# Turning the hidden activations of two MLPs: TensorE transposes against 16-bit transposing DMAs in SBUF

## The reference

```python
def sq_relu_mlp(xn, w_up, w_down):
    return jnp.square(jax.nn.relu(xn @ w_up)) @ w_down

for l in range(DEPTH):
    hn = rms_norm(h, mix_norm_g[l])
    h = h + (diff_hgrn_mixer(...) if l % 2 == 0 else short_conv_mixer(...))
    hn = rms_norm(h, mlp_norm_g[l])
    h = h + sq_relu_mlp(hn, mlp_w_up[l], mlp_w_down[l])
```

## Time and profile before

| | before |
|---|---|
| median of 3 runs (lowest to highest) | 2233.13 us (2233.05 to 2233.82) |
| the profiled execution's own time | 2233.02 us |
| its span (first to last instruction) | 2231.3 us |
| TensorE busy | 2218.5 us, 99% |
| VectorE, ScalarE, GpSimd busy | 82%, 60%, 13% |
| mean granted clock of TensorE | 0.999 |

### The profile page before, as it was taken

How to read it: one execution, slowest core, us unless ns; L and a number is a source line. 1 busy time by engine, 2 the same in 40 slices (tenths; PEclk the granted TensorE clock), 3 DMA queues, 4 the chain that set the end, 5 groups by cost and what they waited for, 6 DMA issues and landing times.

```text
span 2231.3 us, 29958 instructions
## 1 busy us (share of the span) xinstructions
PE 2218.5 (99%) x10290; PEld 1842.1 (83%) x10290; DVE 1831.9 (82%) x1922; ACT 1349.7 (60%) x1708; POOL 290.7 (13%) x413
## 2 busy tenths in 40 slices
PE   9999999999999999999999999999999999999998
PEld 8888888888888888888888888888888888888887
DVE  5778888866888888888876999886888888888886
ACT  6555555537666666666666566565665665665664
POOL 4444555520000000000000000000000000000000
PEclk9999999999999999999999999999999999999999
DMA  9555555566779678678656878757686796796755
GB/s 280 160 167 152 155 164 150 151 180 217 210 250 274 196 248 274 198 246 274 198 170 236 244 227 247 230 159 251 190 293 194 233 293 193 231 296 194 231 180 170
DMA packets 326408, 479.96 MB, mean 215 GB/s; under 512 B 13929, under 2 KB 145810, under 8 KB 319634
## 3 DMA queue, kind: packets, MB, share of 16 engines
q1 hardware_dynamic: 318322, 423.88, 58.0%
q0 software_dynamic: 7344, 53.48, 12.9%
q10 hardware_dynamic: 624, 1.07, 0.1%
HBM read 422.79 MB, written 2.10 MB: 190 GB/s over the span
## 4 chain that ended last, share of the span: by engine, by line
PE 95%; DVE 2%; issue 1%; POOL 1%; ACT 1%; SPq 0%; DMA 0%; POOLq 0%; DVEq 0%; ACTq 0%
PE pair L483 21%; PE pair L485 20%; PE pair L493 20%; PE m L1192 9%; PE m L1183 9%; PE m L1186 9%; PE m L1246 1%; DVE w_lo L599 1%; PE m L1022 1%; PE m L1084 1%; PE m L948 1%; DVE raw L1973 0%; PE m L1036 0%; PE m L1047 0%; PE m L1266 0%
## 5 line engine op out<-in xcount | busy, mean ns | idle before, releaser
L593 ACT ACTIVATE w_hi<-raw 128x1024 fp32r<-128x1024 f32 x796 | 814.4, 1055 | 583.4 <-DVE raw L1973 301.1
L599 DVE TENSOR_TENSOR w_lo<-raw,w_hi 128x1024 fp32r<-128x1024 f32 x796 | 940.1, 1219 | 217.5 <-ACT w_hi L593 213.6
L483 PE MATMUL pair<-w_hi,yT_hi 128*128 128x512 f32 x1264 | 496.2, 393 | 0.0
L485 PE MATMUL pair<-w_hi,yT_lo 128*128 128x512 f32 x1264 | 492.2, 389 | 0.0
L464 DVE TENSOR_TENSOR w_lo<-raw,w_hi 128x1024 fp32r<-128x1024 f32 x208 | 256.0, 1254 | 117.9 <-ACT w_hi L451 116.9
L451 ACT ACTIVATE w_hi<-raw 128x1024 fp32r<-128x1024 f32 x208 | 218.4, 1060 | 221.7 <-PE pair L485 217.1
L493 PE MATMUL pair<-w_lo,yT_hi 128*128 128x512 f32 x1264 | 338.1, 389 | 0.0
L483 PE MATMUL pair<-w_hi,xT_hi 128*128 128x512 f32 x832 | 329.8, 396 | 0.0
L485 PE MATMUL pair<-w_hi,xT_lo 128*128 128x512 f32 x832 | 324.3, 390 | 0.0
L493 PEld LDWEIGHTS pair<-w_lo,yT_hi 128*128 128x128 f32 x1264 | 237.2, 188 | 49.7
L483 PEld LDWEIGHTS pair<-w_hi,yT_hi 128*128 128x128 f32 x1264 | 237.3, 188 | 48.2 <-issue 0.3
(11 more groups left out here) (192 smaller groups left out, 2284.8 us busy)
## 6 DMA issues: line engine op xcount, KB each, us to landing
raw<-in_mlp_w_up SPq DMA_DIRECT2D x128, 1024.0 KB, 7.1
raw<-in_mlp_w_down SPq DMA_DIRECT2D x256, 512.0 KB, 6.4
raw<-in_ab_w_in SPq DMA_DIRECT2D x256, 256.0 KB, 4.1
raw<-raw POOLq DMA_DIRECT2D x51, 1024.0 KB, 8.6
raw<-in_conv_w_in SPq DMA_DIRECT2D x32, 1024.0 KB, 7.0
raw<-in_ab_w_out SPq DMA_DIRECT2D x64, 256.0 KB, 4.5
raw<-in_conv_w_in SPq DMA_DIRECT2D x32, 512.0 KB, 5.7
raw<-in_conv_w_out SPq DMA_DIRECT2D x32, 512.0 KB, 5.8
```

The source lines that it names most:

```text
L483: nc.tensor.matmul(dst[:, tt], at(hi, kt, tt), w_hi[:, ring, q], start=begin, stop=False)
L485: mm = nc.tensor.matmul(dst[:, tt], at(lo, kt, tt), w_hi[:, ring, q], start=False, stop=False)
L593: nc.scalar.activation(w_hi[:, entry % HALVES], src, ACT.Copy).then_inc(hi_ready, 1)
L599: nc.vector.tensor_tensor(w_lo[:, entry % HALVES], src, w_hi[:, entry % HALVES].bitcast(F32), ALU.subtract).then_inc(lo_ready, 1)
```

## The change

The pairs are no longer turned by TensorE. Each block is turned on its own, in SBUF:
- `turn` moves to ScalarE, right after a block's square. An ACTIVATE with Copy reads the block as 16-bit halves of its 32-bit words and writes all lower halves, then all upper halves (`parts`, 128 x 1024 elements of 16 bits). ScalarE waits for its own write and issues one transposing DMA of 128 x 1024 16-bit elements from `parts` to `turned_parts`.
- `hidden_hi` (ScalarE) waits for that DMA, puts the halves together again with a second ACTIVATE (`whole`), waits for that, and rounds the 128 x 512 block into yT_lo's space. The high parts are now in yT_lo and the low parts in yT_hi, as `parts` and `whole` lie over yT_hi, `turned_parts` over yT_lo.
- `hidden_lo` (VectorE) is one subtraction of 128 x 512 per block, from SBUF.
- The places: turn at X3 (C11), X4 (C21, after `hidden_hi` of C11), before round 1 (C12, C22), and at D3, D4, D5, D6 of each round. `hidden_hi` at X4 and X5 ahead of the splits, then in P1 (and D0 in round 1), P4, P2, D7 behind the splits. `hidden_lo` in D5, D6, D7 and the next P1. `copy` of C21 moves from P4, behind the splits, to D4, ahead of the split.
- The waits on c_T are now on c_parts (laid apart). The wait of P2 for c_lo is gone.

The core of the diff:

```diff
-                def turn(r, pair_of):            # TensorE
-                    for at, c in enumerate(pair_of):
-                        n = made(st, r, c)
-                        pe.wait_ge(c_sq, n)
-                        if at == 0 and n > 1:
-                            pe.wait_ge(c_lo, n - 1)
...
-                        for q in range(4):
-                            ins = nc.tensor.transpose(M[turn_bank(r, c)][:, q * P:(q + 1) * P],
-                                                      c_block(st, c)[:, q * P:(q + 1) * P], ident[:])
-                        ins.then_inc(c_T, 1)
...
-                def hidden_hi(r, pair_of):
-                    eng.wait_ge(c_T, made(st, r, pair_of[1]))
-                    low = "C11" if "C11" in pair_of else "C12"
-                    nc.scalar.activation(hidden(yT_hi, r, low), turned_pair(r, low), ACT.Copy
-                                         ).then_inc(c_hi, 2)
+                def turn(r, c):                   # ScalarE
+                    n = made(st, r, c)
+                    eng.wait_ge(c_sq, n)
+                    nc.scalar.activation(
+                        parts(r, c).rearrange("p (s k) -> p s k", s=2),
+                        c_block(st, c).bitcast(U16).rearrange("p (k s) -> p s k", s=2), ACT.Copy
+                        ).then_inc(c_parts, 1)
+                    eng.wait_ge(c_parts, n)
+                    eng.dma_start_transpose(
+                        turned_parts(r, c).rearrange("p (a b) -> p a b", b=P), parts(r, c)
+                        ).then_inc(c_turned[n % 2], 16)
+                def hidden_hi(r, c):
+                    n = made(st, r, c)
+                    eng.wait_ge(c_turned[n % 2], 16 * ((n + 1) // 2))
+                    nc.scalar.activation(
+                        parts(r, c).rearrange("p (k s) -> p s k", s=2),
+                        turned_parts(r, c).rearrange("p (s k) -> p s k", s=2), ACT.Copy
+                        ).then_inc(c_whole, 1)
+                    eng.wait_ge(c_whole, n)
+                    nc.scalar.activation(hidden(yT_lo, r, c), whole(r, c), ACT.Copy
+                                         ).then_inc(c_hi, 1)
...
                     elif p == 3:
                         wait_product(eng, at + 3, 0, 0)
                         square(0, "C11")
+                        turn(0, "C11")
                         square(0, "C21")
+                    if p == 4 and st != CONV:
+                        hidden_hi(0, "C11")
+                        turn(0, "C21")
+                    if p == 5 and st != CONV:
+                        hidden_hi(0, "C21")
...
                 square(0, "C12")
+                turn(0, "C12")
                 square(0, "C22")
+                turn(0, "C22")
...
-                        if name == ("P5" if r == 1 else "D0"):
-                            hidden_hi(r - 1, ("C12", "C22") if r == 1 else ("C21", "C11"))
+                        if name == "D4":
+                            copy(r, "C21")
                         split(slot + 2)
                         if name[0] == "P":
                             split(slot + 3)
-                        if name == "P4":
-                            hidden_hi(r, ("C22", "C12"))
-                            copy(r, "C21")
+                        if name == "P1":
+                            hidden_hi(r - 1, "C12" if r == 1 else "C11")
+                        if name == "D0" and r == 1:
+                            hidden_hi(0, "C22")
+                        if name in ("P4", "P2", "D7"):
+                            hidden_hi(r, {"P4": "C22", "P2": "C12", "D7": "C21"}[name])
...
                         if name in ("D3", "D4", "D5", "D6"):
                             square(r, {"D3": "C22", "D4": "C12", "D5": "C21", "D6": "C11"}[name])
-                hidden_hi(ROUNDS - 1, ("C21", "C11"))
+                            turn(r, {"D3": "C22", "D4": "C12", "D5": "C21", "D6": "C11"}[name])
+                hidden_hi(ROUNDS - 1, "C11")
```

More of the change, by code:

```diff
@@ L30 @@
 U32 = mybir.dt.uint32
+U16 = mybir.dt.uint16
 ALU = mybir.AluOpType
@@ L169, in build @@
             in_y = beside[:, KT * T // 2:]
+            in_y_hi = beside[:]
         yT_hi = sb("yT_hi", [P, KT, T], F32R)
+        with nc.sbuf_tensor("beside_lo", [P, KT * T], F32) as beside_lo:
+            in_y_lo = beside_lo[:]
         yT_lo = sb("yT_lo", [P, KT, T], F32R)
@@ L566, in part_of, with block_at, whole, parts @@
             return half // 2, slice(2 * (half % 2), 2 * (half % 2) + 2)
+        def block_at(r, block):
+            return 4 * (r % 2) + (0 if block in ("C11", "C21") else 2) + int(block in ("C21", "C22"))
         def hidden(tile, r, block):
[L570 to L582, removed]
+            at = 512 * block_at(r, block)
+            return tile.rearrange("p a b -> p (a b)")[:, at:at + 512]
+        def whole(r, block):
+            at = 512 * block_at(r, block)
+            return in_y_hi[:, at:at + 512]
+        def parts(r, block):
+            return whole(r, block).bitcast(U16)
+        def turned_parts(r, block):
+            at = 512 * block_at(r, block)
+            return in_y_lo[:, at:at + 512].bitcast(U16)
+        def hidden_at(tile, kt, tt):
+            at = 512 * (kt // 4 * 2 + tt) + P * (kt % 4)
+            return tile.rearrange("p a b -> p (a b)")[:, at:at + P]
         def c_block(st, block):
@@ L1301, in stage @@
                              p % 4 == 0, p % 4 == 3)
-                    if p == 5 and st != CONV:
-                        turn(0, ("C11", "C21"))
                 if st == CONV:
@@ L1331, in stage @@
                             down(r, int(name[1]))
-                        if name == ("D0" if r == 1 else "P1"):
-                            turn(r - 1, ("C12", "C22") if r == 1 else ("C21", "C11"))
-                        if name == "P4":
-                            turn(r, ("C22", "C12"))
-                turn(ROUNDS - 1, ("C21", "C11"))
                 for m in range(8):
@@ L1590, in stage @@
                         squares(norm, (2 * p - 2, 2 * p - 1))
-                    if p == 6 and st != CONV:
-                        hidden_hi(0, ("C11", "C21"))
                     split(at + p + 2)
@@ L2133, in stage @@
                         sum_squares(norm)
-                    if p == 6 and st != CONV:
-                        hidden_lo(0, ("C11", "C21"))
+                    if p in (5, 6) and st != CONV:
+                        hidden_lo(0, ("C11", "C21")[p - 5])
                     if p == 7 and st == CONV:
```

49 lines of the change are left out of this document (23 added, 26 removed).

## The result

The changed kernel is slower: 2326.97 us median of 4 runs (2325.78 to 2330.25) against 2233.18 of the kernel before in the same session, a ratio of 1.0421 with a 95% interval of 1.0408 to 1.0434. I had forecast 2244 us with a range of 2214 to 2315. The sign was right, the size was not.

The account below looks back on a forecast made before the run. TensorE's own list of work was taken as the bound. Per stage -14.4 (turns) + 4.6 (start) + 7.0 (round 1) + 6 x 1.4 (rounds) = +5.6, two stages +11 on 2233.0: 2244 us, range 2214 to 2315.

Parts of the forecast that it names:

- What bounds it, and the direction: Whole kernel: TensorE's own list of work bounds it, a late ScalarE makes VectorE then TensorE late; slower at 0.60.
- Turns removed, 28.8 us: TensorE, both stages: 32 pairs of blocks at 0.9 us each leave its list, if it never waits.
- Laying apart 1.06: ScalarE, per block: the 16-bit strided ACTIVATE of 1024 elements takes 1.06 us, like a w_hi half.
- Laying together 1.06: ScalarE, per block: the copy that puts the halves together again takes 1.06 us.
- Rounding 0.58: ScalarE, per block: rounding to yT_lo after the halves are put together takes 0.58 us.
- Issue 0.86: ScalarE, per block: issuing the transposing DMA holds it 0.86 us, with 0.34 and 1.66 as ends.
- rival 2: ScalarE's queue: the issue holds it 1.66 us or more and ScalarE becomes the bound, 2293 us; chance 0.32.
- D5, 1.2 lost: Each steady round at D5's first half: ScalarE has 3.6 us more ahead, against a margin of 2.4, 1.2 lost.
- D6 to P5 fits: Each steady round, D6 to P5: two turns and three blocks laid together need 9.1 of ScalarE's 13.1 us idle.
- Landing 6.4, hidden in rounds: Transposing DMA: lands 6.4 us from issue; C21's and C11's transfers have about 12 us in a round, so hidden.
- rival 3: Transposing DMAs: landing is the bound at 10.9 us or more, blocks queuing with weight loads, 2264 us; chance 0.08.
- The granted clock at 1.00: TensorE: granted clock left at 1.00, though stops of 3 us are twice the trace's longest.

Follow-up runs that it names:

- bare copies: Changed kernel without any DMA, the laying apart made one 32-bit ACTIVATE of 128x512 and the laying together left out: 2219.5 us, ratio 0.9938.
- second pair without a DMA: Changed kernel with the transposing DMAs of C21 and C11 left out in rounds 1 to 7: 2300.7 us, ratio 1.0297.

## Why the prediction was wrong

By spans, the 94.3 us between before (2231.3) and after (2325.6) are: turns removed, with bare copies, -13.6; 16-bit copies +21.1; transfers on SyncE's queue +6.9, at the stage starts, round 1 and the ends; the issue on ScalarE instead of SyncE +79.9.

1. *What bounds it, and the direction*: right. A late ScalarE made VectorE and TensorE late, at the places named: X6, D0 of round 1, D5. Over half of TensorE's 82 us of idle time are waits for w_hi.
2. *Turns removed, 28.8 us*: a pair is 0.9 us of TensorE's list as I had it (a round's matmuls alone are 81.6). What failed is that the gain arrives: P6 took back 0.9 a round in the bare kernel, where I had 0.2, because I priced the wait by its idle time alone. A stop also delays the matmuls behind it by some 0.3 us: at D5 the second comes 2.03 us late (1001.30, where matmuls 0.23 us apart would have had it at 999.27), of which the idle time is 1.75.
3. *Laying apart 1.06*: right, 1.058. *Laying together 1.06*: mis-sized, 1.36; it writes in steps of two elements, the other only reads so. *Rounding 0.58*: 0.63.
4. *Issue 0.86*: this is the step that decided. It takes 1.25 us, with the pause behind it 1.38. I took the row of the nearest route, GpSimd's; but that was another engine and a plain pattern, and the number that I kept as an end (1.66) was no farther off. From 1.1 up my own rival 2 was to hold, and it does. What it lost before the turns are taken off was 4.6 us a round, 10.4 in round 1, 6.1 at the start and 0.5 at the end; measured in the same way (0.9 us added per pair) it is 6.4, 12.7, 3.9 and 4.5, so its start was too dear and all else too cheap.
5. *D5, 1.2 lost*: 1.75 idle and 0.3 behind it. The formula was fair: with the measured 1.06 + 0.03 + 1.38 it gives 1.9 + 0.48 + 2.47 - 0.25 - 2.4 = 2.2.
6. *D6 to P5 fits*: false. The second pair without a DMA shows 1.2 us a round, most of it the stop in P5. I had compared sums of work with sums of idle time, 9.1 against 13.1 us; by my own terms it is 9.0 (two turns of 1.95, three times 1.7), and in rival 2 10.6 plus a backlog of 5 would overflow 13.1 by 2.5, where I had 1.5 without a reason. VectorE's work ahead of the sums for P5 counts as well: with its subtraction on GpSimd the 0.28 us stop in P5 is gone and a round is 0.7 us shorter (both with the issue on SyncE), while a later half of P5 still starts 0.53 us behind the matmul before it, as in the other. That a delay of VectorE there is paid in full is argued and not shown.
7. *Landing 6.4, hidden in rounds*: right, 7.0. The longest is 13.9. ScalarE waits for a landing four times in all, 3.9 and 3.8 us in X4 and 0.6 and 1.0 at the ends, so rival 3 is out. The estimate of 10.5 us from the page "VectorE: DVE Perf Modes" of the Trainium skill is not borne out: a block of eight squares lands in 7.0, one of four in 6.1 and the plain transfer in 6.1.
8. *The granted clock at 1.00*: wrong after some of the stops. TensorE around 2.03 us without a matmul at X6, and the window of it with the granted clock as the third number from the right:

```profile
565.11 1.07 PE L499 MATMUL pair<-w_lo,xT_hi 128*128 128x512 f32 x4
568.21 0.68 PE L489 MATMUL pair<-w_hi,xT_hi 128*128 128x512 f32 x1 [2.03 <-ACT w_hi L457]
568.68 0.63 PE L491 MATMUL pair<-w_hi,xT_lo 128*128 128x512 f32 x1
569.11 0.63 PE L489 MATMUL pair<-w_hi,xT_hi 128*128 128x512 f32 x1
...
567.00:572.00 5.00, 3.79 (x10) 3.01 (x11) 3.74 (x4) 4.97 (x7) 0.00 (x0) 0.66 0.05 10
```

Matmuls start 0.43 us apart instead of 0.23, which is the level of 1.2 GHz, for some 3.5 us, and the window's granted clock is 0.66. The same follows the 3.9 us stop at D0 of round 1. The length of the stop does not decide alone. In this trace the clock fell in six places: after stops of 2.03, 3.89, 1.82, 3.99, 1.78 and 3.63 us. It stayed at its upper level (1.00) after one of 2.03 us at 647.91, one of 3.43 at 1208.48, and those of 1.7 to 1.85 us at D5 of rounds 2 to 7. Over the whole span the granted clock is 0.994 against 0.999, which makes 0.005 x 2326 = some 12 us of the 94 at most, an estimate, a term that I had set to zero though the stops were in my own sum. With the issue on SyncE it is 0.999 again.

So the step that failed is the issue's length (0.86 for 1.25 to 1.38), which put the case on the side of rival 2; the P5 stretch, the price behind a stop and the clock made it larger still (2327 against the 2293 that I had for that rival). Moving the issue alone gives 79.9 of the 94.3 us back. The form of the loss, a late ScalarE at the places named, was right; the direction was too, though I gave the case that came only 0.32.

## What to carry to other kernels

An engine with 40% idle time has none where its halves are due: look for what stands between two successive deadlines, and ask who issues each DMA, as moving 64 issues from ScalarE to SyncE gave back 79 of 94 us here. Where an unknown price has a threshold in its range, find it and weigh the cases by that, rather than by the nearest row. Price a stop of TensorE at its idle time plus some 0.3 us, and keep apart what the lower clock may cost behind it: in this case 3.5 us of matmuls at half speed after some stops of 1.8 us and more, and nothing after others as long.

## What the runs showed of the hardware

- A transposing DMA from SBUF to SBUF holds its issuing engine 1.25 us, 1.21 at half the size; a plain one of the same bytes 0.47. One issued about 3 us after another took 1.9 to 3.7 us on ScalarE's queue in six rounds and 1.25 in the seventh; SyncE's took up to 6.1 among weight loads.
- A 16-bit ACTIVATE Copy of 128x1024 takes 1.06 us with strided reads and 1.36 with strided writes.
- A GpSimd subtraction of 128x512 from SBUF took 1.3 us at the median, and 9.84 beside subtractions and sums of VectorE that followed each other without a pause. The page "SBUF — State Buffer" of the Trainium skill (section "SBUF: two separate sides") says that the two engines share a pair of ports, held for a whole instruction, also by a VectorE operation with two inputs from SBUF; the trace agrees, and adds that successive VectorE instructions let GpSimd wait until there is a pause.
- TensorE's clock fell to its lower level after stops of 1.78, 1.82, 2.03, 3.63, 3.89 and 3.99 us, and not after one of 2.03, one of 3.43 and those of 1.7 to 1.85 at D5 of rounds 2 to 7.
- A wait of under 0.1 us of idle time delayed TensorE's matmuls by some 0.35 us in all.
